# A two-block transformer kernel on one core: GpSimd's subtractions of 1024 columns are issued as four of 256

## What is computed

```python
for l in range(2):
    x = x + 0.5 * swiglu(rms_norm(x, ffa_norm[l]), ffa_w_in[l], ffa_w_out[l])   # 2816 wide
    h = rms_norm(x, mix_norm[l])
    parts = split_cols(h @ w_in[l], IN_SPLITS)
    o_mla, o_gdn, o_moba = mla_branch(...), gdn_branch(...), moba_branch(...)
    up = einsum('bsnw,nwd->bsnd', stack([o_mla, o_gdn, o_moba]), w_branch[l])
    x = x + sum(sigmoid(gate_logits) * up) @ w_out[l]
    x = x + 0.5 * swiglu(rms_norm(x, ffb_norm[l]), ffb_w_in[l], ffb_w_out[l])
```

## Time and profile before

| | |
|---|---|
| median of 3 runs | 2853.03 us (2852.99 to 2853.11) |
| span of the profiled execution, first to last instruction | 2852.2 us |
| busy: TensorE, VectorE, ScalarE, GpSimd | 89%, 34%, 31%, 36% |
| the two layers | 1172 to 2852 us of the span |
| GpSimd's subtractions | 424, 1027.3 us |

### The profile page before, as it was taken

How to read it: one execution, slowest core, us unless ns; L and a number is a source line. 1 busy time by engine, 2 the same in 40 slices (tenths; PEclk the granted TensorE clock), 3 DMA queues, 4 the chain that set the end, 5 groups by cost and what they waited for, 6 DMA issues and landing times. The chain is left out here.

```text
span 2852.2 us, 37927 instructions
## 1 busy us (share of the span) xinstructions
PE 2534.9 (89%) x15142; PEld 1826.0 (64%) x15142; DVE 973.9 (34%) x1514; ACT 888.3 (31%) x1266; POOL 1027.5 (36%) x428
## 2 busy tenths in 40 slices
PE   8889999999999998799778976899799777986899
PEld 3544443434434343599767866899799767875898
DVE  0322121212222121311465775221211557774221
ACT  1311212111111211444344531343444444431342
POOL 0000000000000000488548521688688546522686
PEclk9889999999999999899889997999899888997999
DMA  8249999999999995455325320354455324311453
GB/s 333 97 180 428 429 428 428 429 428 429 427 430 427 430 428 243 134 185 185 133 68 170 103 75 30 132 185 157 161 186 185 123 86 136 119 60 40 153 187 138
DMA packets 94236, 650.66 MB, mean 228 GB/s; under 512 B 10448, under 2 KB 12416, under 8 KB 68128
## 3 DMA queue, kind: packets, MB, share of 16 engines
q1 hardware_dynamic: 94112, 648.94, 58.8%
HBM read 647.84 MB, written 1.06 MB: 228 GB/s over the span
## 5 line engine op out<-in xcount | busy, mean ns | idle before, releaser
L489 POOL TENSOR_TENSOR w_lo<-raw,w_hi 128x1024 fp32r<-128x1024 f32 (+3 forms) x424 | 1027.3, 2446 | 1807.5 <-ACT w_hi L483 1807.5
L1319 PE MATMUL bank<-ring,scratch 128*64 128x512 f32 x3072 | 686.1, 596 | 27.2 <-DMA ring<-in_expert_units 25.4
L483 ACT CAST w_hi<-raw 128x1024 fp32r<-128x1024 f32 (+3 forms) x424 | 419.8, 1038 | 672.0 <-PE bank L506 659.6
L504 PE MATMUL bank<-hT_hi,w_hi 128*128 128x256 f32 x1984 | 566.1, 285 | 18.6 <-ACT scratch L1762 9.5
L505 PE MATMUL bank<-hT_lo,w_hi 128*128 128x256 f32 x1984 | 565.0, 285 | 0.0
L506 PE MATMUL bank<-hT_hi,w_lo 128*128 128x256 f32 x1984 | 564.9, 285 | 0.0
L1319 PEld LDWEIGHTS bank<-ring,scratch 128*64 128x64 f32 x3072 | 209.7, 137 | 455.0 <-issue 386.7
L504 PEld LDWEIGHTS bank<-hT_hi,w_hi 128*128 128x128 f32 x1984 | 384.8, 194 | 21.6 <-issue 10.5
L505 PEld LDWEIGHTS bank<-hT_lo,w_hi 128*128 128x128 f32 x1984 | 384.8, 194 | 0.8
L506 PEld LDWEIGHTS bank<-hT_hi,w_lo 128*128 128x128 f32 x1984 | 384.5, 194 | 0.0
L1487 DVE TENSOR_TENSOR scratch<-bank,scratch 128x512 f32<-128x512 f32 x64 | 44.3, 692 | 605.0 <-PE bank L1333 601.1
(11 more groups left out here) (263 smaller groups left out, 2832.8 us busy)
## 6 DMA issues: line engine op xcount, KB each, us to landing
ring<-in_expert_units SPq DMA_DIRECT2D x192, 2048.0 KB, 20.5
raw<-in_layer_units SPq DMA_DIRECT2D x408, 512.0 KB, 4.7
ring<-in_first_units SPq DMA_DIRECT2D x6, 2048.0 KB, 23.9
ring<-in_ple_units SPq DMA_DIRECT2D x2, 2048.0 KB, 9.9
raw<-in_layer_units SPq DMA_DIRECT2D x8, 424.0 KB, 3.4
raw<-in_layer_units SPq DMA_DIRECT2D x4, 384.0 KB, 3.2
const<-in_const SPq DMA_DIRECT2D x1, 1184.0 KB, 7.3
x_res<-in_x SPq DMA_DIRECT2D x1, 1024.0 KB, 4.9
```

What stands on the lines that cost most here:

```text
L483: k.nc.scalar.copy(k.w[0][i % SPLIT_SLOTS][:, at], k.raw[n % RAW_SLOTS][:, 0:at.stop - at.start]).then_inc(k.sem("weights_hi"), 1)
L489: k.nc.gpsimd.tensor_tensor(k.w[1][i % SPLIT_SLOTS][:, at], k.raw[n % RAW_SLOTS][:, 0:at.stop - at.start], k.w[0][i % SPLIT_SLOTS][:, at], ...
L504: nc.tensor.matmul(out, lhsT[0], rhs[0], start=start, stop=False)
L1319: last = nc.tensor.matmul(b[g * SL:(g + 1) * SL, :], lhsT[:, c, :], w[:, c, g, :], start=start and c == 0, stop=stop and c == 3)
```

## The change

`lo_pool` issues four subtractions where it issued one, each on a quarter of the piece's columns: 256 of 1024, 212 of 848, 192 of 768, 128 of 512. The wait for ScalarE's cast stands before the first of the four; `weights_split` is raised by the last alone. The values written are the same.

```diff
@@ -76,6 +76,7 @@
 RAW_SLOTS, SPLIT_SLOTS = 4, 3
+LO_PARTS = 4
 
@@ -486,8 +487,13 @@
 def lo_pool(k, pool, i):
     for n, at in pieces(i):
         pool.wait_ge(k.sem("weights_hi"), n + 1)
-        k.nc.gpsimd.tensor_tensor(k.w[1][i % SPLIT_SLOTS][:, at], k.raw[n % RAW_SLOTS][:, 0:at.stop - at.start],
-                                  k.w[0][i % SPLIT_SLOTS][:, at], ALU.subtract).then_inc(k.sem("weights_split"), 1)
+        words = at.stop - at.start
+        for j in range(LO_PARTS):
+            own = slice(j * words // LO_PARTS, (j + 1) * words // LO_PARTS)
+            to = slice(at.start + own.start, at.start + own.stop)
+            last = k.nc.gpsimd.tensor_tensor(k.w[1][i % SPLIT_SLOTS][:, to], k.raw[n % RAW_SLOTS][:, own],
+                                             k.w[0][i % SPLIT_SLOTS][:, to], ALU.subtract)
+        last.then_inc(k.sem("weights_split"), 1)
```

## The result

The changed kernel takes 2907.86 us (median of 4 runs, 2903.92 to 2913.84) where the kernel before, on the same chip, takes 2853.07 (4 runs, 2852.99 to 2853.72): 1.0192 times as long, with an interval of 1.0178 to 1.0206. It is **slower by 55 us**, outside the predicted range. The profiled execution spans 2911.6 us, 59.4 more than the one before.

The account below looks back on a forecast made before the run. TensorE's pace bounds the feed-forward, GpSimd next; in the mixer TensorE waits for VectorE chains that GpSimd slows. Gains 2.7 + 4.6 + 1.0 + 2.4 less 1.3 and 2.5 give 6.9 us a layer, 13.8 in all: 2839.2 us, range 2828 to 2879.

Parts of the forecast that it names:

- A short piece in sequence, 0.70 us: GpSimd subtractions of 256 columns follow each other after 0.70 us, bounds 0.65 and 0.78; four take 2.80 us for 2.36.
- three rivals: Other short-piece prices: 0.69 or less, 2834 us (chance 0.12); 0.715, a wash, 2854 (0.16); from 0.72, slower, 2879 to 2919 (0.27).
- A turn, 0.56 us: A VectorE operation waiting behind one 256-column GpSimd piece is delayed 0.56 us, bounds 0.5 and 0.7.
- L629, "Nothing. If that cover went, 1.2 us each.": Feed-forward subtraction into act_lo: shorter waits in 44 places gain nothing, being covered by one TensorE step of over 10 us.
- First feed-forward, loss 2.5; second, 0: GpSimd's short pieces and turns, summed against when TensorE wants the last half: 2.5 us lost in the first block, 0 in second.
- Before the first attention, gain 2.7: VectorE's chain L647 to L667: 15 short waits, 8.4 us, replace five long ones, 11.1 us; gain 2.7 us a layer.
- Before the second, 4.6: Before the second attention: VectorE's chain ends earlier, TensorE's weights then limit, L309 starts at 1560.0 for 1564.64; gain 4.6 us.
- Convolution, loss 1.3: Convolution: GpSimd delivers a half each 7.7 us beside VectorE's turns, so TensorE ends at 1654.4 for 1653.10; loss 1.3 us.
- Output projection, gain 1.0: Output projection: four L1843 take 4.7 us for 6.79, but the L1847 behind them wait two turns; gain 1.0 us.
- Norms, gain 2.4: Norms: L205 waits half a short piece, taking about 0.5 us for 1.68, twice a layer; gain 2.4 us.
- Rival 4: Head norm and convolution mainly: VectorE gets no turn between short pieces and waits out the burst; 2910 us, chance 0.05.
- rival 3: Feed-forward parts: from 0.72 us a short piece GpSimd becomes the bound; 2879 us at 0.74, 2919 at 0.78; chance 0.27.

Follow-up runs that it names:

- e3: Changed kernel with the feed-forward's product left in PSUM, so the subtraction into act_lo has one SBUF input; 2865.6 us, ratio 1.0044 to the kernel before.
- e2: Changed kernel (four parts) with GpSimd waiting until each part has ended before it issues the next; 2956.6 us.
- e12: Changed kernel (four parts) with GpSimd waiting for the fourth part's end, once per piece; 2886.5 us.
- e4: Changed kernel with whole pieces in both feed-forward parts and four parts only in the mixer; 2859.8 us, ratio 1.0015 to the kernel before.
- e9: Changed kernel with each piece of 1024 columns cut into parts of 256, 256 and 512 instead of four quarters; 2847.9 us.
- e14: Kernel before (whole pieces) plus one extra GpSimd subtraction of 320 columns per half, its result overwritten; 2940.2 us.
- e7: Changed kernel (four parts) with an already met semaphore wait ahead of the second, third and fourth part; 2913.6 us.
- e13: Changed kernel with two parts instead of four, plus one extra GpSimd subtraction of 192 columns per half, its result overwritten; 2917.2 us.
- e5: Changed kernel with four parts only for halves 36 to 45, two for 46 to 57, whole pieces elsewhere; 2842.12 us, ratio 0.9958 to the kernel before.
- e11: Changed kernel with four parts only for halves 58 to 69, beside and just behind the convolution, whole pieces elsewhere; 2864.1 us.
- e15: Changed kernel (four parts) with GpSimd waiting for its own last part once in a half; 2872.2 us.

## Why the prediction was wrong

Point by point, by its own steps:

- *A short piece in sequence, 0.70 us.* Right: 0.697. The room between its bounds, on which three rivals and 0.55 of the chances hung, did not matter. What mattered is what 0.70 does to GpSimd's **pause**. Before, it idled 34 times in the first feed-forward block; after, 5 times (the rows of its line between 1172 and 1380, the idle time in sum and in times; 1172 us of each are the first block):

```profile
  ACT w_hi L483: 1203.1, 34
```

```profile
  ACT w_hi L484: 1183.7, 5
```

- *A turn, 0.56 us.* Right in size wherever VectorE was let in: L669 takes 1.21 us for 0.69. Wrong as a law: it holds near the start of a stream and inside a run of VectorE operations, and not for one that comes late into a long stream.
- *L629, "Nothing. If that cover went, 1.2 us each."* **This is the step that failed.** It took for granted that L629 always gets the next turn. 20 of the 44 took over 3 us, up to 25.9 (and not all had taken 2.45 before: four took 1.06). The cover of 10 us, one step of TensorE, was too short for 15, and ScalarE's casts behind L626 had no cover at all.
- *First feed-forward, loss 2.5; second, 0.* Measured 19.1 and 6.3. Without VectorE's wait (e3) they lose 0.8 and 3.0, 3.8 together for the 2.5 of the capacity sum.
- *Before the first attention, gain 2.7*, with the norm's share: 5.7 in the first layer, 3.7 in the second. *Before the second, 4.6*: 1.2, because L650 waited 17.57 us. With two parts and no lockout it was 3.7.
- *Convolution, loss 1.3*: 0.7. The step stopped at L755. What GpSimd owed there, the pieces that it had ready at 1663.2 before and has ready at 1678.5 now, came due behind it: ScalarE's casts without loads, and L1033 behind them, 7.61 us at TensorE, and 9.7 us up to TensorE's transposes of the gated delta rule's result (L841). The prediction said that "waits, casts and transfers stay", and never asked who frees a raw buffer.
- *Output projection, gain 1.0*: 1.1. *Norms, gain 2.4*: the one behind the projection lost 2.1, its L206 taking 2.80 us for 1.68. It had come 19 us into a stream and waited for its end: the same lockout.
- *Rival 4*, "VectorE gets no turn between short pieces and waits out the burst", stood at 0.05 and at 2910 us. Its time is near the measured one by chance only: it put 26 us a layer into the head norm and the convolution, where VectorE mostly had its turns, and 2.5 into the feed-forward blocks, where it lost 25. I ruled it out with the earlier trace rows, where both long bursts alternate. Those rows show a VectorE that is already taking turns. None shows an operation that comes from idleness 10 us into a stream; there was none.

That GpSimd is the bound of the feed-forward (rival 3) is shown for e2 and e12, not for the changed kernel: in e3 it does the same pieces for a loss of 0.8 and 3.0 us in the two blocks.

What stays open: why a long stream shuts VectorE out. The limit is not sharp. The earliest arrivals that were kept out came 7.5 (e4) and 8.7 us (e9) into a stream, while four at 18 to 19 us (e14) and one at 24 us (e9) were let in. Nor does a lockout always last to the stream's end: the first subtraction into `act_lo`, 25 us into a stream, was let in after 7.1 to 7.2 us in the changed kernel and at the same place in e7, e13 and e14, with GpSimd going on. The GpSimd operations grow from some 0.73 to 0.78 us in width within a stream while their spacing stays 0.70; whether that has to do with it was not tried. Nor was a fifth raw buffer; that the loads come late through GpSimd rests on the waits and on e5 and e11.

## What to carry to other kernels

When two engines take turns, look at the pause that the busier one leaves as well as at the length of its operations: a change that costs it 18% of its pace (5.58 us a half for 4.75) can cost the other its turn altogether. Ask of every queue that falls behind what it frees and for whom, past the place where its own output is next needed. And a row in which two engines alternate says nothing about an operation that arrives alone; look for one that does, and if there is none, give the unseen case a chance.

## What the runs showed of the hardware

- A stream of GpSimd subtractions with no pause can hold a VectorE operation with two SBUF inputs off, mostly until the stream ends: up to 25.2 us ahead of 0.69 us of work (changed kernel), and 14.5 us with operations of 1024 columns (e14). The Trainium skill, SBUF — State Buffer, section "SBUF: two separate sides", says that whichever operation starts first holds the shared pair for the whole instruction while the other blocks. The trace agrees for arrivals early in a stream (mostly up to 0.6 us behind a short piece); by that rule alone the one at 1220.18 would have waited under 1 us, and it waited 14.4.
- A pause of 0.12 us once in 5.6 us is enough to end this (e15); a wait that is already met is not (e7).
- The same operation with its first input in PSUM is not touched at all: 0.691 to 0.694 us in 44 places (e3).
- Two-input subtractions on GpSimd follow each other after 0.697 us at 256 columns, 0.885 at 341 and 1.256 at 512.
